# Chunk stage of an RWKV-7 branch: heads' 64x64 products in two alternating layouts over the array's four quarters, level sums accumulated in PSUM

## The reference, cut to what matters

```
sa = S @ a_t                               # a_t = -kk, b_t = kk * a
S  = S * w_t + outer(sa, b_t) + outer(v_t, k_t)
y  = S @ r_t
```

## Time and profile before

| | us |
|---|---|
| median of 3 runs (lowest to highest) | 1297.88 (1296.78 to 1299.94) |
| the profiled execution's own time | 1300.64 |
| its span, first to last instruction | 1298.7 |
| chunk stage, scores of round 0 to the last s | 138.5 to 306.1 |
| PE busy, share of the span | 1208.4 (93%) |
| DVE, ACT, POOL busy | 426.7 (33%), 317.8 (24%), 93.6 (7%) |

### The profile page before, as it was taken

One profiled execution on the slowest core, in us unless ns is written; L12 is line 12 of the kernel. 1 busy time (PEld: TensorE's weight loads), 2 busy tenths in 40 slices (PEclk: granted clock), 3 DMA queues, 4 the chain that ended last, 5 costly groups with the idle time before them and its releaser, 6 DMA issues.

```text
span 1298.7 us, 24268 instructions
## 1 busy us (share of the span) xinstructions
PE 1208.4 (93%) x10798; PEld 888.3 (68%) x10798; DVE 426.7 (33%) x750; ACT 317.8 (24%) x530; POOL 93.6 (7%) x132
## 2 busy tenths in 40 slices
PE   8999999999999999999999998999888888888895
PEld 8899998988798889999999786333333333333332
DVE  5347622336164535333333224112111111111116
ACT  5454322334333533222222231000000000000004
POOL 2000000000100100000000002111111111111100
PEclk9989989999999999999999999999999998999998
DMA  7210102110332643233233657999999999999996
GB/s 238 66 33 1 35 6 68 44 60 21 118 100 71 183 175 98 74 84 88 74 102 142 246 222 291 420 418 419 420 419 420 419 420 419 420 420 419 419 420 217
DMA packets 113426, 283.30 MB, mean 218 GB/s; under 512 B 23779, under 2 KB 71093, under 8 KB 88746
## 3 DMA queue, kind: packets, MB, share of 16 engines
q1 hardware_dynamic: 107546, 269.93, 55.0%
q0 software_dynamic: 5120, 9.46, 1.9%
q10 hardware_dynamic: 656, 2.36, 0.4%
HBM read 273.44 MB, written 15.60 MB: 223 GB/s over the span
## 4 chain that ended last, share of the span: by engine, by line
PE 68%; DMA 16%; SPq 7%; DVE 6%; issue 1%; ACT 1%; DVEq 0%; ACTq 0%
DMA slot<-in_e_wu_dram 15%; PE bank L1427 8%; PE bank L646 7%; SPq L595 7%; PE bank L1365 6%; PE bank L1367 6%; PE bank L1366 6%; PE bank L653 4%; PE bank L1487 2%; PE bank L1488 2%; PE bank L1489 2%; PE bank L1638 2%; PE bank L1642 2%; PE bank L1640 1%; PE bank L1600 1%
## 5 line engine op out<-in xcount | busy, mean ns | idle before, releaser
L646 PE MATMUL bank<-slot,xs 128*64 128x512 f32 x512 | 249.8, 638 | 59.6 <-DMA slot<-in_e_wu_dram 58.6
L647 PE MATMUL bank<-slot,xs 128*64 128x512 f32 x512 | 250.8, 641 | 0.0
L646 PEld LDWEIGHTS bank<-slot,xs 128*64 128x64 f32 x512 | 70.2, 145 | 203.4 <-issue 200.3
L1365 PE MATMUL bank<-xnh,wh 128*128 128x256 f32 (+1 forms) x448 | 133.1, 297 | 0.6 <-DVE mt L2920 0.6
L1367 PE MATMUL bank<-xnh,low 128*128 128x256 f32 (+1 forms) x448 | 132.6, 296 | 0.0
L1366 PE MATMUL bank<-xnl,wh 128*128 128x256 f32 (+1 forms) x448 | 132.6, 296 | 0.0
L872 ACT ACTIVATE sg<-bank 64x512 f32<-64x512 f32 x32 | 19.0, 594 | 445.0 <-PE bank L647 445.0
L1001 DVE TENSOR_TENSOR xs<-bank,g2x 128x512 f32<-128x512 f32 x32 | 22.1, 692 | 315.9 <-PE bank L770 315.9
L653 PE MATMUL bank<-slot,ht 128*64 128x512 f32 x512 | 117.1, 598 | 1.0 <-DVE ht L1029 0.5
L2503 DVE TENSOR_TENSOR low<-ring,wh 128x1536 fp32r<-128x1536 f32 (+1 forms) x45 | 89.9, 2005 | 79.4 <-ACT wh L2144 72.0
L1365 PEld LDWEIGHTS bank<-xnh,wh 128*128 128x128 f32 x448 | 85.0, 190 | 1.3 <-issue 1.2
(11 more groups left out here) (503 smaller groups left out, 2269.1 us busy)
## 6 DMA issues: line engine op xcount, KB each, us to landing
slot<-in_e_wg_dram SPq DMA_DIRECT2D x64, 1024.0 KB, 27.7
slot<-in_e_wu_dram SPq DMA_DIRECT2D x64, 1024.0 KB, 27.9
slot<-in_e_wd_dram SPq DMA_DIRECT2D x64, 1024.0 KB, 28.3
ring<-in_w_in_dram SPq DMA_DIRECT2D x13, 1024.0 KB, 5.3
ring<-in_w_in_dram SPq DMA_DIRECT2D x24, 512.0 KB, 4.2
ring<-in_w_branch_dram SPq DMA_DIRECT2D x24, 256.0 KB, 4.6
kvs<-in_cache_mem_k_dram SPq DMA_DIRECT2D x8, 512.0 KB, 5.8
kvs<-in_cache_mem_v_dram SPq DMA_DIRECT2D x8, 512.0 KB, 5.9
```

The lines of the kernel that those rows point to most:

```text
L646: pe.matmul(out[64:128, :], tok, wg[:, FF * k:FF * k + FF], start=(k == 0), stop=(k == KD - 1))
L647: mm = pe.matmul(out[0:64, :], tok, wu[:, FF * k:FF * k + FF], start=(k == 0), stop=(k == KD - 1))
L1365: pe.matmul(part, w_h, xh_(k, cols), start=(k == 0), stop=False)
```

## The change

Per chunk (the samples keep their products as they were):

- Products are issued by `each_quarter` in groups of four, one on each quarter of the array. A product may leave a head on the other half of the partitions, so heads have two layouts: level n reads one and writes the other, and after level 4 they are back in the first. Rows 0 to 63 write one PSUM bank, rows 64 to 127 its neighbour. Three things stay on the diagonal by `each_head`: level 5, and x's and y's products with the state.
- X's sum is made in PSUM: in levels 0 to 4 an identity product adds X (at level 0 the identity). Level 0 so makes two products for X that DVE made by one addition before. ACT now copies the three results of one bank and DVE those of the other bank, 384 columns each, in place of 512 on ACT and 256 on DVE.
- The keys' part of x is made early, beside the turned keys (`turn_kt`), copied by ACT to `xa`, and added to x by DVE (`x_row`); y's product with the state has a bank of its own, is copied by ACT (`yst`), and DVE adds the rest of y to it before it updates the state.
- Order: each state step stands between the levels of the two chunks of a pair; scores of a chunk wait for the last level of the chunk before it in its lane; the keys' scores move to level 2 (3 in round 0); the samples' x, its turning and u move from round 1 to round 0, their y to the start of round 1; one bonus product of the normalisation moves from level 3 to level 5 of round 4.
- SP waits for DVE's y of chunks 2, 3 and 4 in place of ACT's. POOL makes doubled masks (`low2`, `up2`) before the stage.

The diff cut to its core (removed lines stand in the kernel above; "..." marks what is left out):

```diff
+xa = [sb(f"xa{n}", [128, NB, C], F32, e1_at + at) for n, at in enumerate((6144, 5120))]
...
+    dve_st.wait(sp, ("y", u - 6))
...
+def each_quarter():
+    for j in range(2):
+        yield [(2 * j + k, slice(64 * p, 64 * p + 64), slice(64 * k, 64 * k + 64), p, k, 2 * p + j, j)
+               for p, k in ((0, 0), (1, 1), (0, 1), (1, 0))]
...
+def chunk_scores(c):
+    a = place_of[c][1]
+    for quarter in each_quarter():
+        for b, q, k, p, _, _, j in quarter:
+            pe.matmul(two_units(2 * a + p, k, 0, j), bb[q, b, C * c:C * c + C], ra[q, b, c, :, :], start=True, stop=True)
+        for b, q, k, p, _, _, j in quarter:
+            mm = pe.matmul(psum[2 * a + p][k, 256 + C * j:256 + C * j + C], ra[q, b, c, 1, :], bb[q, b, C * c:C * c + C],
+                           start=True, stop=True)
+    pe_c[a].done(mm, ("m", c))
...
+    for a, c in enumerate(PAIRS[it]):
+        o = before_in_lane(c)
+        act_c[a].wait(pe, ("p", o, levels_of[o] - 2))
+        dve_c[a].wait(pe, ("level", o, levels_of[o] - 1))
+        if o == SMP:
+            act_st.wait(pe, ("u", SMP))
+        chunk_scores(c)
...
 def level(c, n):
+    if c == SMP:
+        sample_level(n)
+        return
     a, t, last = place_of[c][1], sx[set_of[c]], levels_of[c] - 1
     if n == 0:
         dve_c[a].wait(pe, ("mt", c))
     else:
         act_c[a].wait(pe, ("p", c, n - 1))
...
+        dve_c[a].wait(pe, ("level", c, n - 1))
+    if n == last:
+        for b, q in each_head():
+            mm = pe.matmul(head(2 * a + 1, q, b), t[q, 2, b, :], t[q, 3, b, :], start=True, stop=True)
+        pe_c[a].done(mm, ("level", c, n))
+        return
+    for quarter in each_quarter():
+        heads_ = [(k, s_, psum[2 * a + kk][q, :], j) if n % 2 == 0 else (q, b, psum[2 * a + p][k, :], j)
+                  for b, q, k, p, kk, s_, j in quarter]
+        if n < last - 1:
+            for r, s_, out, j in heads_:
+                pe.matmul(out[:, C * j:C * j + C], t[r, 2, s_, :], t[r, 1, s_, :], start=True, stop=True)
+        for r, s_, out, j in heads_:
+            pe.matmul(out[:, 128 + C * j:128 + C * j + C], t[r, 1, s_, :], t[r, 2, s_, :], start=True, stop=True)
+        for r, s_, out, j in heads_:
+            x = t[r, 3, s_, :] if n else i64[r, :]
+            pe.matmul(out[:, 256 + C * j:256 + C * j + C], t[r, 2, s_, :], x, start=True, stop=False)
+        for r, s_, out, j in heads_:
+            x = t[r, 3, s_, :] if n else i64[r, :]
+            mm = pe.matmul(out[:, 256 + C * j:256 + C * j + C], i64[r, :], x, start=False, stop=True)
+    pe_c[a].done(mm, ("level", c, n))
...
+def key_scores(it, cs):
+    act_turn.wait(pe, ("vbs", it) if it else ("kt", SMP))
+    for c in cs:
+        a = place_of[c][1]
+        for quarter in each_quarter():
+            for b, q, k, p, _, _, j in quarter:
+                mm = pe.matmul(two_units(4 + p, k, 256 * a, j), pt[q, NB + b, C * c:C * c + C], ra[q, b, c, :, :],
+                               start=True, stop=True)
+        pe_c[a].done(mm, ("mk", c))
+def turn_kt(it, cs):
+    for c in cs:
+        dve_c[place_of[c][1]].wait(pe, ("mk", c))
+    for c in cs:
+        a, n = place_of[c][1], set_of[c]
+        for quarter in each_quarter():
+            for b, q, k, p, _, _, j in quarter:
+                pe.matmul(psum[4 + p][k, 256 * a + C * j:256 * a + C * j + C], pt[q, NB + b, C * c:C * c + C], i64[q, :],
+                          start=True, stop=True)
+            for b, q, k, p, kk, s_, j in quarter:
+                mm = pe.matmul(psum[4 + kk][q, 256 * a + 128 + C * j:256 * a + 128 + C * j + C], rkm[n][k, 1, s_, :],
+                               vb[n][k, 0, s_, :], start=True, stop=True)
+    pe_turn.done(mm, ("kts", it) if it else ("kt", 0))
...
+def x_of(c):
+    if c == 1:
+        act_st.wait(pe, ("sn", NB - 1))
+    dve_st.wait(pe, ("s", c - 1))
     for b, q in each_head():
...
+        mm = pe.matmul(head(6, q, b), ra[q, b, c, 1, :], st[q, b, :], start=True, stop=True)
     pe_st.done(mm, ("x", c))
...
     for b, q in each_head():
...
+        mm = pe.matmul(head(7, q, b), st[q, b, :], ra[q, b, c, 0, :], start=True, stop=True)
+    pe_st.done(mm, ("yst", c))
...
+def u_of(c):
+    dve_c[place_of[c][1]].wait(pe, ("level", c, levels_of[c] - 1))
+    if c == 0:
+        act_turn.wait(pe, ("kt", 0))
+        act_r.wait(pe, ("row", 3))
+    else:
+        dve_st.wait(pe, ("x", c))
+        act_st.wait(pe, ("yst", c))
+    for quarter in each_quarter():
+        for b, q, k, p, kk, _, j in quarter:
+            x = xt[q, b, :] if c else xa[1][q, 2 * kk + j, :]
+            mm = pe.matmul(psum[6 + p][k, 256 + C * j:256 + C * j + C], sx[set_of[c]][q, 3, b, :], x, start=True, stop=True)
     pe_st.done(mm, ("u", c))
...
+def y_and_s(c):
     n = set_of[c]
...
+    act_st.wait(pe, ("u", c))
+    act_turn.wait(pe, kt_turned(c))
+    for quarter in each_quarter():
+        for b, q, k, p, kk, s_, j in quarter:
+            pe.matmul(psum[6 + kk][q, 384 + C * j:384 + C * j + C], vb[n][k, 0, s_, :], rkm[n][k, 0, s_, :], start=True, stop=False)
+        for b, q, k, p, kk, s_, j in quarter:
+            mm = pe.matmul(psum[6 + kk][q, 384 + C * j:384 + C * j + C], ut[k, s_, :], sx[n][k, 0, s_, :], start=False, stop=True)
     pe_st.done(mm, ("y", c))
...
+    for quarter in each_quarter():
+        for b, q, k, p, kk, s_, j in quarter:
+            pe.matmul(psum[6 + kk][q, C * j:C * j + C], kt[n][k, s_, :], vb[n][k, 0, s_, :], start=True, stop=False)
+        for b, q, k, p, kk, s_, j in quarter:
+            mm = pe.matmul(psum[6 + kk][q, C * j:C * j + C], vb[n][k, 1, s_, :], ut[k, s_, :], start=False, stop=True)
     pe_st.done(mm, ("s", c))
...
+        elif n == 3:
+            dve_st.wait(pe, ("s", 0))
+            sample_s(0, 6)
+            sample_s(1, 7)
+        elif n == 5:
+            act_st.wait(pe, ("sn", 0))
+            sample_s(2, 6)
+            act_st.wait(pe, ("sn", 1))
+            sample_s(3, 7)
+    else:
...
+            (x_of, u_of, y_and_s)[n % 3](prev[n // 3])
...
+    if pair_ and it >= 2:
+        turn_vb(it, pair_)
...
+    if it == 1:
+        act_turn.wait(pe, ("kt", 0))
+        sample_y(5)
...
+    if pair_ and n < levels_of[pair_[0]]:
+        level(pair_[0], n)
+    state_step(it, n)
+    if len(pair_) > 1:
+        level(pair_[1], n)
+    if pair_:
...
+    x0 = 1 if n < levels_of[c] - 2 else 2
+    to = t[:, x0:4, 0:4:2, :] if n % 2 == 0 else t[:, x0:4, 0:2, :]
+    last = act.activation(to, psum[2 * a][:, 128 * x0 - 128:384].rearrange("p (x j n) -> p x j n", j=2, n=C), ACT.Copy)
...
+def chunk_masks(c):
+    a, t = place_of[c][1], sx[set_of[c]]
+    pe_c[a].wait(dve, ("m", c))
+    dve_c[a].done(dve.tensor_tensor(t[:, 2, :, :].rearrange("p (q j) n -> p q (j n)", j=2), banks8[:, 2 * a:2 * a + 2, 256:384],
+                                    low_twice, ALU.mult), ("m", c))
+    dve_c[a].done(dve.tensor_tensor(across(t[:, 0:2, :, :]),
+                                    banks8[:, 2 * a:2 * a + 2, 0:256].rearrange("p q (x m) -> p q x m", x=2), up_twice,
+                                    ALU.mult), ("mt", c))
...
 def grown(c, n):
...
+    a, t = place_of[c][1], sx[set_of[c]]
     pe_c[a].wait(dve, ("level", c, n))
...
+    if n == levels_of[c] - 1 or c == SMP:
+        dve_c[a].wait(dve, ("mk", c) if (c, n) == (SMP, 1) else ("level", c, n - 1))
+        last = dve.tensor_tensor(t[:, 3, :, :], t[:, 3, :, :], heads3(psum[2 * a + 1][:, 0:256]), ALU.add)
+    else:
+        x0 = 1 if n < levels_of[c] - 2 else 2
+        to = t[:, x0:4, 1:4:2, :] if n % 2 == 0 else t[:, x0:4, 2:4, :]
+        last = dve.tensor_copy(to, psum[2 * a + 1][:, 128 * x0 - 128:384].rearrange("p (x j n) -> p x j n", j=2, n=C))
+    dve_c[a].done(last, ("level", c, n))
...
+def x_row(c):
+    pe_st.wait(dve, ("x", c))
+    act_turn.wait(dve, kt_turned(c))
+    dve_st.done(dve.tensor_tensor(by_bank(xt[:, :, :]), psum[6][:, 0:256].rearrange("p (j q n) -> p q j n", q=2, n=C),
+                                  xa[place_of[c][1]][:, :, :].rearrange("p (q j) n -> p q j n", j=2), ALU.add), ("x", c))
+def y_and_s(c):
+    y_ = by_bank(o_rw[:, :, C * c:C * c + C])
     pe_st.wait(dve, ("s", c))
...
     if c == 0:
...
+        end = wcp[:, :, c].rearrange("p (j q) -> p q j", q=2).unsqueeze(3).to_broadcast([128, 2, 2, C])
+        dve_st.done(dve.tensor_copy(y_, pair_of(384)), ("y", c))
+        dve_st.done(dve.tensor_tensor(by_bank(st[:, :, :]), pair_of(0), end, ALU.mult), ("s", c))
     else:
...
+        act_st.wait(dve, ("yst", c))
+        dve_st.done(dve.tensor_tensor(y_, y_, pair_of(384), ALU.add), ("y", c))
+        seq(dve.tensor_tensor(by_bank(st[:, :, :]), by_bank(st[:, :, :]), pair_of(0), ALU.add))
+        dve_st.done(dve.tensor_tensor(st[:, :, :], st[:, :, :], over_i(wcp[:, :, c]), ALU.mult), ("s", c))
...
+    for a, c in enumerate(pair_):
+        if a == 1:
+            state_step(it, n)
+        if (1 if c == SMP else 0) <= n < levels_of[c]:
             grown(c, n)
...
```

(49 more changed lines are left out.)

507 lines of the change are left out of this document (246 added, 261 removed).

## The result

The changed kernel takes 1303.63 us (20 runs), the kernel before 1299.63 us beside it (20 runs). The ratio is 1.0036, with a 95% interval of 1.0025 to 1.0048: slower by about 4 us, where 30 us faster was forecast. The profiled execution took 1303.3 us of its own, with a span of 1301.5.

The account below looks back on a forecast made before the run. PE was taken to bound the chunk stage, with the expert-weight stream following it. 38.2 us of PE work less 6 of waits and 2 of blocks gave 30.2 us, 1300.64 to 1270.4, median 1267.7, said as 1268; range 1258 to 1286.

Parts of the forecast that it names:

- The pace on four quarters: Identity-product burst on PE: 14.6 ns per record on four quarters against 29.0 on two, carrying the forecast.
- the rival that doubted it: Quarters don't serve different operands at once, or the gain is lost: within 0.3%, 1298 us; chance 5%.
- the 38.2 us: PE's products in eight chunks: 13.8 us per chunk becomes 9.0, 38.2 us less in all.
- the one on instruction blocks: PE's blocks of 256 instructions, one every 1.9 us instead of 3.7: 2 us added, bounds 0 and 6.
- it binds wholly: Issue of PE's records in levels 0 to 4, at 29 ns per record: slower, about 1323 us; chance 9%.
- My own sign for it: PE's records in a level's windows at 20 ns or more would point to the sequencer.
- The evacuations: Copies of 384 columns out of PSUM: about 0.49 us on ACT and 0.56 on DVE, costing nothing by volume.
- The 6 us of exposed waits: PE idle at round ends and in rounds 0, 4 and 5: 6 us of new waits, bounds 0 and 12.
- the x of chunk 7 behind the weight split on DVE: Round 5: x now needs DVE, busy with a last product and a 2.29 us weight split: 1.8 us.
- The end follows the stage: A microsecond taken from PE's chunk stage starts the expert-weight stream, and ends the run, a microsecond earlier.

Follow-up runs that it names:

- the long series: Kernel before plus 960 identity products near the start, on four, two and one quarters; the four-quarter part took 28.8 us.
- the two shortened versions: Changed kernel with P squared and P times X joined in levels 1 to 3: 1297.97 us; changed kernel with P + 1 made by DVE: 1293.25 us.
- quiet series: Kernel before with identity products added near the start, or after the last s, where little is loaded; no total time given.

## Why the prediction was wrong

**The pace on four quarters was right.** I took 14.6 ns from a burst of 48 records; the changed stage runs at 14.5 and the long series at 14.7. Different operands serve four quarters as well as one operand does, and the rival that doubted it is out.

**Most of the 38.2 us were there, and became idle time.** PE's busy time fell by 28.9 us. Of the other 9 the lower clock of the stage, 0.94 in place of 0.98, is 0.06 x 170 - 0.02 x 168 = 7 us by estimate. At full clock a burst is as short as predicted, and what it gains is waited away behind it.

**The step that failed is the one on instruction blocks.** I wrote that on four quarters a block is used every 1.9 us instead of 3.7, "With blocks twice as often I add 2 us (bounds 0 and 6)". The arithmetic of the blocks was right and the price was a guess: the trace of before shows six blocks in 20 us of narrow products, one in some 3.5 us, and nothing faster. The burst that carried the pace could not show it: 48 records and 48 loads are 96 instructions, less than half a block. Measured in its place: one block in 3.3 to 3.9 us when DMA is quiet (3.46 in the long series), 6.5 to 7.1 us where weights are loaded at some 320 to 370 GB/s, and 32.4 us of idle time on "issue" in the stage against 2.8 before, 29.6 more where I had added 2. The two "issue" waits of 1.4 us beside weight loads were this same wait. I saw where they fell and did not ask what they would be at twice the demand. The upper bound should have been a supply no faster than the one seen in use. Rounds 2 and 3 of before hold 3590 records of both kinds (14.0 blocks) in 58.8 us; after they hold 4395 (17.2 blocks). At the 3.7 us that a block takes on two quarters that is 64 us, and 65.2 were measured, where I had forecast 38 to 42.

**Why it is slower, and not only the same.** Where the blocks bind, what counts is instructions. The change adds 48 products per chunk, 384 in all, 1536 instructions or six blocks; at the 2.6 to 2.7 us per block that the two shortened versions gave back, six blocks are 16 us, and stretches of the stage that were the array's and not the supply's pay for some 12 of them. This split is argued from those two runs and not measured by itself. The clock is another candidate that no run separates: over whole executions it was granted at 0.970 on average in the changed kernel and 0.976 in the kernel before, at most 0.006 x 1300 = 8 us by estimate. It doesn't explain what the shortened versions gave back, which ran at 0.970 and 0.967.

**The rival "it binds wholly" had the sign and the place, the issue of PE's records in levels 0 to 4, but the wrong mechanism.** It has no price per record. It asked for 25 ns or more between records and gave 1323; the records come at 14.5 ns and then not at all. My own sign for it ("records at 20 ns or more") would have cleared it, had only the pace in full windows been looked at. The Trainium skill's floor of about 25 ns between the starts of matmuls ("TensorE: Matmul & The Clock Gate", section "Wait — 56ns, not 53.3ns?") is not seen here: 14.7 ns over 128 records.

The Trainium skill, "Runtime: NRT & Kernel Launch", section "Instruction fetch mechanics", states that instructions are refilled in blocks of 256 and that the cost of crossing a block is mostly hidden. The bursts of exactly 128 records and 128 loads agree with the block; the 1.3 to 5.0 us of idle time behind bursts at full clock, and 0.9 and 2.8 behind those at half, do not agree with the second half. In the kernel before, with its two gaps of 1.4 us in the stage, the trace did agree.

**The waits were sized too high.** The evacuations have the price I gave them (columns: line, engine, names, shapes, count, busy us and mean ns, idle time before and its releaser):

```profile
L2853 DVE COPY sx<-bank 128x384 f32<-128x384 f32 x32 | 17.8, 557 | 63.0 <-PE bank L1705 63.0
L2373 ACT ACTIVATE sx<-bank 128x384 f32<-128x384 f32 x32 | 15.7, 491 | 47.8 <-PE bank L1705 47.8
```

0.56 and 0.49 us were taken. The 6 us of exposed waits are nearly absent, probably because PE waits for its blocks in the same time. One place came as described, the x of chunk 7 behind the weight split on DVE, though the profile puts the gap down to "issue", so that 1.8 of the 32.4 us are not the supply's:

```profile
302.21 2.28 DVE L2656 TENSOR_TENSOR low<-ring,wh 128x2048 fp32r<-128x2048 f32 x1
...
304.41 0.42 DVE L2865 TENSOR_TENSOR xt<-bank,xa 128x256 f32<-128x256 f32 x1
...
304.93 0.46 PE L1797 MATMUL bank<-xt,sx 64*64 64x64 f32 x16 [1.79 <-issue]
```

**The end follows the stage.** The first product after the last y (L1878) starts at 308.12, 2.0 us later than before, and the first product of the next branch at 320.06, 3.5 us later (316.60 before). Between them the clock is lower; the window from 310 to 320 us, after (first row) and before (second):

```profile
310.00:320.00 10.00, 9.84 (x94) 9.03 (x94) 2.55 (x7) 2.38 (x6) 0.00 (x0) 0.66 0.07 15
```

```profile
310.00:320.00 10.00, 10.00 (x95) 8.73 (x95) 3.48 (x6) 4.69 (x11) 0.00 (x0) 0.84 0.07 15
```

So of these 3.5 us more than half is the stage, and the rest goes with the lower clock behind it (0.34 x 10 - 0.16 x 10 = 1.8 us by estimate); the profiled executions differ by 2.7 us in all and don't allow a finer split.

## What to carry to other kernels

Count the instructions of a stage beside its array time: in these traces TensorE gets 256 of them in about 3.5 us, and in about 7 us while DMA loads at over 300 GB/s, so products that take under some 27 ns per MATMUL-and-LDWEIGHTS pair for longer than a block are paid in instructions and no longer in array time. Here PE had "issue" gaps with the same number of records between them; spreading the work over more of the array brought nothing, but joining products that share weights, and moving an addition from PE to an engine with slack, did. A short burst can't price this: a pace has to be read over more than one block. A price that no row shows should be bounded by the fastest pace that a row does show, here the supply of instructions as much as the array.

## What the runs showed of the hardware that I had not expected

- Instructions of PE arrive 256 at a time, 3.46 us apart in quiet series and 3.3 to 3.9 in the changed stage, 6.5 to 7.1 us under heavy loads. Two loaded intervals, three quiet ones in the series and five in the stage are what is shown here. The transfer of a block starts 1.1 us after PE has started on the last one in quiet stretches, and some 4 us after in the loaded ones.
- PE starts products of other quarters while older ones wait for theirs: 16.5 ns per record with an order written in twos.
- 64x64 float32 products take 58.6, 29.0 and 14.7 ns per MATMUL record on one, two and four quarters.
- The clock was lower behind gaps: behind the 5.00 us gap the burst ran at 0.50 and took 3.69 us instead of 2.09. The stage as a whole was granted 0.94 after and 0.98 before. That the gaps are the cause was not tried by itself.
- A fulfilled wait on a semaphore is not free to PE: two semaphore instructions and a product took 0.24 us at a clock of 0.50, a product alone 0.06.
- A product of one column, written ahead of a product to the same place with the same weights, cost 0.08 to 0.11 us, more than the 0.058 us of a product of 64 columns on two quarters.
